# Two stage changes of a two-block network, worked in token halves

## The reference

```
# block 1
h = rms_norm(x) * gain * (1 + sc1) + sh1
y = hybrid_mixer(h)                       # gated convolution beside attention, then @ w_o
x = x + g1 * rms_norm(y, mix_post_g)      # stage change 1 begins with this line
h = rms_norm(x, ffn_pre_g) * (1 + sc2) + sh2
y = swiglu_ffn(h)                         # (silu(h @ wg) * (h @ wu)) @ w_ffn_out
x = x + g2 * rms_norm(y, ffn_post_g)      # stage change 2 begins with this line
# block 2
h = rms_norm(x, norm_g) * (1 + scale) + shift
y = mamba2_mixer(h)                       # h @ in_w, causal convolution, state space, @ out_w
...                                       # then an attention block and a last norm
```

## Time and profile before

| | |
|---|---|
| median of 3 runs | 1399.63 us (1399.52 to 1403.42) |
| the profiled execution | 1405.93 us, its span 1404.1 us |
| TensorE busy | 1342.2 us (96%) |
| VectorE / ScalarE / GpSimd busy | 823.6 (59%) / 588.5 (42%) / 407.2 (29%) |
| TensorE's granted clock over the run | 0.973 of full |
| DMA | 181 MB, mean 129 GB/s |

### The profile page before, as it was taken

The page is one execution under the profiler, slowest core; times in us unless marked ns, Lnnn a source line. Parts: engine busy times, 40 slices in busy tenths (PEclk is TensorE's granted clock), DMA queues, the critical chain, the costliest instruction groups (busy, mean ns, idle before and its releaser), DMA issues. The chain is left out here.

```text
span 1404.1 us, 19406 instructions
## 1 busy us (share of the span) xinstructions
PE 1342.2 (96%) x7840; PEld 1068.1 (76%) x7840; DVE 823.6 (59%) x966; ACT 588.5 (42%) x849; POOL 407.2 (29%) x191
## 2 busy tenths in 40 slices
PE   5999999889999999999999999999999999999996
PEld 3778867668888888887778886777786799777775
DVE  2789974476655654323766665777842842566644
ACT  4323646333222222112454347867732422455551
POOL 0000000039988888999100000000000050233310
PEclk9999999979999999999799999999999899999998
DMA  9434052215454445554132334333322342111121
GB/s 385 145 146 150 31 208 96 87 34 204 171 219 179 179 179 183 210 180 185 51 130 84 104 115 121 113 113 102 117 90 91 123 169 89 70 50 42 61 91 60
DMA packets 41350, 181.12 MB, mean 129 GB/s; under 512 B 3392, under 2 KB 20160, under 8 KB 21312
## 3 DMA queue, kind: packets, MB, share of 16 engines
q1 hardware_dynamic: 40128, 171.73, 33.9%
q10 hardware_dynamic: 1152, 8.39, 1.8%
HBM read 173.75 MB, written 6.36 MB: 128 GB/s over the span
## 5 line engine op out<-in xcount | busy, mean ns | idle before, releaser
L193 DVE TENSOR_TENSOR wlo<-raw,whi 128x2048 fp32r<-128x2048 f32 x95 | 257.1, 2707 | 172.0 <-ACT whi L189 169.4
L200 POOL TENSOR_TENSOR ada_raw<-ada_raw,cs 128x2048 f32<-128x2048 f32 x36 | 144.6, 4018 | 495.2 <-DVE h2lo L454 446.9
L271 PE MATMUL ps<-hhi,whi 128*128 128x512 f32 x640 | 252.0, 394 | 2.4 <-PEq L566 0.8
L271 PE MATMUL ps<-hhi,wlo 128*128 128x512 f32 x640 | 249.4, 390 | 0.0
L271 PE MATMUL ps<-hlo,whi 128*128 128x512 f32 x640 | 249.1, 389 | 0.0
L189 ACT ACTIVATE whi<-raw 128x2048 fp32r<-128x2048 f32 x95 | 181.6, 1911 | 141.7 <-PE ps L1315 91.3
L209 POOL TENSOR_TENSOR ada_raw<-ada_raw 128x1024 f32<-128x1024 f32 x72 | 166.0, 2305 | 5.6
L271 PEld LDWEIGHTS ps<-hhi,whi 128*128 128x128 f32 x640 | 120.2, 188 | 28.7 <-issue 2.4
L271 PEld LDWEIGHTS ps<-hhi,wlo 128*128 128x128 f32 x640 | 120.1, 188 | 25.6
L271 PEld LDWEIGHTS ps<-hlo,whi 128*128 128x128 f32 x640 | 120.3, 188 | 24.4
L2054 POOL TENSOR_TENSOR x<-x,rest 128x256 f32<-128x256 f32 (+3 forms) x32 | 49.1, 1533 | 153.2 <-DVE rest L2349 153.2
(11 more groups left out here) (374 smaller groups left out, 2760.6 us busy)
## 6 DMA issues: line engine op xcount, KB each, us to landing
raw<-panels SPq DMA_DIRECT2D x87, 1024.0 KB, 4.9
ada_raw<-ada SPq DMA_DIRECT2D x48, 1024.0 KB, 6.7
first<-ada SPq DMA_DIRECT2D x8, 1024.0 KB, 20.2
bc<-ac_rows SPq DMA_DIRECT2D x32, 256.0 KB, 3.7
raw<-panels ACTq DMA_DIRECT2D x8, 1024.0 KB, 5.0
x_kept<-x SPq DMA_DIRECT2D x2, 2048.0 KB, 9.5
x<-x_kept SPq DMA_DIRECT2D x2, 2048.0 KB, 8.3
x<-x_in SPq DMA_DIRECT2D x1, 2048.0 KB, 10.3
```

The costliest lines, as they stand in the source:

```text
L193: e.tensor_tensor(wlo[:, c % 2, :, :], raw[:, c % 2, :, :], whi[:, c % 2, :, :].bitcast(F32), ALU.subtract).then_inc(lo_split, 1)
L200: e.tensor_tensor(ada_raw[:, c % 2, :, :], ada_raw[:, c % 2, :, :], cs[:, which, :].unsqueeze(2).to_broadcast([P, KT, 256]), ALU.mult).the ...
L271: mm = e.matmul(ps[:, 2 * (qc % 2) + b, :], w[:, c % 2, 2 * k + b, :], src[part][:, k, :], **flags)
```

## The change

`post_norm` and `pre_norm` at the two stage changes are replaced by one function, `boundary`, that works over tokens 0 to 255 (a = 0) and then 256 to 511 (a = 1). Tiles 7 and 6 of the last panel stay whole; the other six are done for half 0 first and then for half 1, so 72 products of 256 columns stand for 36 of 512. Squares, sums, root, reciprocal and spread exist per half; four `keep` operations of 256 tokens are VectorE's, the six of half 1 ScalarE's. The scale and add steps handle two tiles of 256 tokens at once. The first **two** panels of the next stage are both in `boundary`: panel A half 0, panel B half 0 (with the second norm's sums and spread of half 1 between its products), panel A half 1, panel B half 1, 192 products of 256 columns. ScalarE rounds panel B in four parts between its `high` steps; VectorE's `split_lo` of panel B stands behind its `norm(0)`. The next blocks therefore begin with the third panel. The modulation columns are grouped 4, 4, 5 instead of 3, 3, 1, 1, 2, 3, the last five behind the last product.

```diff
+            def on_pe(pe, part, c, qc):
+                for j in range(2):
+                    part(TILES[j], slice(0, S)).then_inc(N["bank_done"], 1)
+                for j in range(2, KT):
+                    part(TILES[j], HALF[0]).then_inc(N["bank_done"], 1)
+                    for t in {4: (0, 1), 6: (2, 3, 4)}.get(j, ()):
+                        sums(pe, 0, t)
+                for j in range(2, KT):
+                    pe.wait_ge(*no("kept", j + 1))
+                    part(TILES[j], HALF[1]).then_inc(N["bank_done"] if j < KT - 1 else panels_used, 1)
+                    for t in {2: (5, 6, 7)}.get(j, ()):
+                        sums(pe, 0, t)
+                    for t in {3: (0, 1), 6: (2, 3, 4, 5)}.get(j, ()):
+                        sums(pe, 1, t)
+                    if j == 4:
+                        half_spread(pe, 0, 0, 7)
+                for t in (6, 7):
+                    sums(pe, 1, t)
+                columns(pe, 0)
+                half_spread(pe, 1, 1, 6)
+                for i in range(4):
+                    sums2(pe, 0, i)
+                columns(pe, 1)
+                half_spread(pe, 2, 0, 5)
+                pe.wait_ge(*no("x_new1", 2))
+                for a in range(2):
+                    for p in range(2):
...
+                            pe.wait_ge(lo_split, cp + 1)
...
+                            if (a, p) == (0, 1) and k == 3:
+                                for i in range(4):
+                                    sums2(pe, 1, i)
+                            if (a, p) == (0, 1) and k == 6:
+                                half_spread(pe, 3, 1, 7)
+                        if a == 1:
+                            mm.then_inc(panels_used, 1)
+                columns(pe, 2)
...
+                for k in range(KT):
+                    high(0, k)
+                    if k < 4:
+                        split_hi_part(act, last + 2, k)
+                for i in range(4):
+                    square2(1, i)
+                std(1, 7, 12)
+                for k in range(KT):
+                    high(1, k)
...
+                recip(1, 1)
+                dve.wait_ge(*no("spread", 2))
+                scale(1, 0, both(y, 0, 1))
+                recip(2, 0)
+                dve.wait_ge(*no("kept_b", 2))
+                scale(1, 1, both(y, 1, 1))
+                dve.wait_ge(*no("spread", 3))
+                dve.wait_ge(*no("x_new0", 2))
+                dve.wait_ge(*no("x_new1", 2))
+                norm(0)
                 split_lo(dve, last + 2, 0)
...
+                scale(1, 3, both(y, 3, 1))
+                add(1, 3, both(y, 3, 1))
+                recip(3, 1)
+                dve.wait_ge(*no("spread", 4))
...
+                norm(1)
...
                     def _(pe):
-                        pairs(pe, FT - 1, lambda i, r: (in_panel(pe, c0 + 1 + r, q0 + 1 + r, i, (hhi, hlo), False),
+                        pairs(pe, FT - 2, lambda i, r: (in_panel(pe, c0 + 2 + r, q0 + 2 + r, i, (hhi, hlo), False),
                                                         ada_columns(pe, a0 + r, i)))
+                        ada_columns(pe, a0, FT // 2 - 1)
...
-                        xbc_panel(0, 0)
                         xbc_panel(0, 1)
```

More of the change, by code:

```diff
@@ L371, in post_norm, with half_sums, sums @@
-            a0, a1, sums, parts = late or (0, 0, None, [0] * 6)
+            def half_sums(pe, a, bank, src, first, final):
+                for i in range(2):
+                    b = 2 * a + i
+                    mm = pe.matmul(ps[32 * b:32 * b + 32, bank, 0:P], ones[:, 0:32], src[:, i * P:(i + 1) * P], start=first,
+                                   stop=final, skip_group_check=True)
+                return mm
+            def sums(pe, a, j):
+                if j == 0:
+                    pe.wait_ge(*no("kept", a + 1))
+                pe.wait_ge(*no("sq_ready", j + 1 if j < 2 or a == 0 else j + 7))
+                half_sums(pe, a, 7 - a, sq[:, j % 3, HALF[a]], j == 0, j == KT - 1).then_inc(N[sums_of[a]], 1)
@@ L372, in post_norm @@
+            a0, a1, acc, parts = late or (0, 0, None, [0] * 3)
             assert sum(parts) == a1 - a0
@@ L415, in on_dve @@
+                for j in range(2):
+                    keep(j, slice(0, S))
+                split_lo(dve, last + 1, 0)
+                for j in range(2, KT):
+                    keep(j, HALF[0])
+                recip(0, 0)
                 dve.wait_ge(*no("kept", KT))
                 dve.wait_ge(*no("spread", 1))
-                for j, k in enumerate(ORDER):
-                    part = ps[:, SPARE[j], :] if j % 2 else y[:, k, :]
-                    dve.tensor_tensor(part, y[:, k, :], ps[:, ORDER[0], :], ALU.mult).then_inc(N["scaled"], 1)
-                    if j % 2:
-                        dve.wait_ge(*no("scaled", j + 1))
-                        dve.tensor_tensor(x[:, k, :], x[:, k, :], part, ALU.add).then_inc(N["x_new1"], 1)
@@ L1257, in _ @@
                             ada_reduce(pool, a, 0, sums(a))
[L1258 removed]
+                        step2["pool"](pool)
                     @block.scalar
```

266 lines of the change are left out of this document (179 added, 87 removed).

## The result

| | median | lowest to highest | profiled execution |
|---|---|---|---|
| before, 4 runs | 1399.58 us | 1398.45 to 1403.42 | 1405.93, span 1404.1 |
| after, 4 runs | 1436.36 us | 1435.42 to 1442.86 | 1436.47, span 1434.7 |

The ratio is 1.0268 [1.0232, 1.0304]: slower. The forecast was 1424.9 with a range of 1413 to 1434; the direction was right, and the range missed by 2.4 us. Between the two profiled executions the change costs 30.5 us, where 25.3 was forecast.

A forecast was written before the change was run, and what follows sets the result against it. TensorE sets the time nearly everywhere, its clock dipping at both stage changes. Stage change 1 (-1.1 panels, +10.7 idle, +2.4 clock = +12.0) and stage change 2 (+13.3) give +25.3 on 1399.6: 1424.9 us, range 1413 to 1434.

The forecast's parts named there:

- The restart: TensorE behind the new hole at each stage change: the clock falls and must rise again, +2.4 us, bounds 0 and 2.7.
- (1): Sign: first product of the next stage 5 to 8 us sooner after the last panel's start.
- (3): Sign: end of the second panel within 3 us of before, counted from the start of the last panel.
- (2): Sign: TensorE gaps behind panel B's `split_lo` and in panel A half 1, released by VectorE.
- (4): Sign: TensorE idle 10 to 11 us at the feed-forward block's start, 11 to 12 at the next, clock 0.5 after each.
- (5): Sign: the rest of the trace is merely shifted.
- Stage change 2 by the same steps: Panels end at 711.9, columns to 713.1, TensorE starts at 725.5 against 714.64: +10.9, clock +2.4, together +13.3 us.
- The step from the profile to the median: Before's profile is 6.3 us above its median, so +25.3 was added to 1399.6 instead, giving 1424.9 us.
- (a): Rival: no hold, ScalarE and VectorE run on once panel A is done; +6.6 to +11, 1406 to 1411 us; chance 4%.
- (b): Rival: faster or level, as the second panel's time was slack; 1396, with the clock up 1394 us; chance 3%.
- (c): Rival: hold, but TensorE well fed, panels end at 309.9; +7.2 per change, 1414 to 1415 us; chance 14%.
- (d): Rival: worse feeding, small operations and four roots dearer; +3 to +4.5 per change, 1431 to 1434 us; chance 12%.

The follow-up runs named there:

- before again: The kernel before, unchanged, profiled a second time; 1405.5 us.
- before, third and fourth profile, without the dip: The kernel before, unchanged, profiled twice more; the clock did not fall near 197 us; 1400.48 and 1400.24 us.
- after, second profile, without the dip: The kernel after, unchanged, profiled again; the clock did not fall near 197 us; 1433.46 us.
- border_moved: Kernel before, no halves, with only the second panel moved to the old block's end at both stage changes; 1430.23 us, ratio 1.0184.
- one_panel: Kernel after with panel B whole and back in the new block, the rest still in halves; 1416.38 us, ratio 1.0104.
- split_in_old_block: Kernel after with ScalarE's and VectorE's split of the third panel done in the old block; 1427.97 us.
- sums_ahead: Kernel after with the second sums of half 0 ahead of half 1's spread in TensorE's queue; 1437.22 us, ratio 1.0254.
- one_panel_sums_ahead: The queue edit of sums_ahead put on one_panel; 1411.29 us, ratio 1.0083.
- split_and_sums: The queue edit of sums_ahead put on split_in_old_block; 1428.51 us.
- one_panel_early_half: One-panel form, sums ahead, with the second half's norm brought under the first half's products; 1418.73 us, ratio 1.014.
- columns_late: Kernel after with the first two parts of the modulation columns moved behind the last product; one execution, 1439.2 us.
- after_hold_filled: Kernel after with 42 and 46 products of no use at the head of the two new blocks; 1430.55 us, ratio 1.0195.
- before_filled: Kernel before with 36 and 9 products of no use in TensorE's waits inside the two stage changes; 1397.74 us, ratio 0.997.
- experiment 10: The experiment that ran after_hold_filled, to see what the low clock costs; 1430.55 us.
- experiment 8: New profiles of unchanged kernels to test the clock's dip near 197 us: before 1400.48 and 1400.24 us, after 1433.46 us.

## Why the prediction was right or wrong

The stretches of the profiles not in the first table, in us, worked out from the four starts and the span:

| | start to keep 1 | keep 1 to silu | silu to keep 2 | keep 2 to memset | memset to end |
|---|---|---|---|---|---|
| before again | 261.5 | 44.4 | 352.8 | 44.2 | 700.8 |
| before, third and fourth profile, without the dip | 258.5, 258.1 | 44.7, 44.6 | 352.8, 352.8 | 43.1, 43.1 | 699.7, 700.0 |
| after, second profile, without the dip | 257.7 | 55.6 | 353.0 | 60.6 | 704.8 |
| border_moved | 261.2 | 55.3 | 353.8 | 54.7 | 704.6 |
| one_panel | 257.8 | 48.2 | 352.8 | 51.3 | 701.0 |
| split_in_old_block | 261.0 | 55.4 | 349.9 | 60.6 | 701.6 |
| sums_ahead | 261.1 | 54.4 | 353.8 | 61.9 | 702.7 |
| one_panel_sums_ahead | 257.2 | 44.8 | 352.8 | 49.1 | 701.1 |
| split_and_sums | 257.2 | 54.3 | 351.2 | 61.3 | 698.9 |
| one_panel_early_half | 261.0 | 48.3 | 354.2 | 49.5 | 701.7 |
| columns_late | 259.8 | 58.2 | 353.8 | 63.8 | 701.8 |
| after_hold_filled | 257.8 | 55.6 | 352.0 | 62.2 | 700.4 |
| before_filled | 259.1 | 41.1 | 352.8 | 42.4 | 699.8 |

*What held.* The reading that decides the sign: all engines are held at a block's end until TensorE is done, and the second panel was the cover for what follows. `border_moved` shows it with whole panels: 25.9 of the 30.5 us between profiles, its span 1429.6 against 1403.7 for the second profile of before. At stage change 1 the sums of the forecast came out. Brought to the same keep 1, the first product came at 285.3 (forecast 284.6), the end of the panels at 315.2 (314.7), the third panel's first matmul at 325.8 (325.4). All of it, up to keep 2, cost 11.2 + 0.4 = 11.6 us, with 12.0 forecast.

Part of that agreement is luck. The root behind the last sum, forecast at 276.1, starts at 277.9 on that scale (276.58, 16.4 us after keep 1), 1.8 late; the last product of the old stage ends at 275.8 and not at 273.9. Then 1.1 came back: the forecast has the sums and the spreads behind that root at the lower clock, and in this execution the clock stayed at the upper level until 283. Where it fell in time, in stage change 1 of `columns_late`, the first product is 3.3 us later than the steps say (26.45 for 23.15 after keep 1). The restart was too dear in the forecast as well: up to keep 2 only 1.6 us are left for it, where 2.4 was forecast, and filling the hole gave 1.0 to 1.2 back (experiment 10). And the rise at stage change 2 was misread: 0.67 in the microsecond from 694 puts it at 694.7, 6.0 and not 5.7 us after the first product, which changes the 2.4 by less than 0.1.

Of the signs named, (1), the first product 5 to 8 us sooner, holds at stage change 1 (5.6) and fails at stage change 2 (2.2). (3), the panels' end within 3 us of before, holds at both, 0.6 sooner and 2.2 later. (2) holds for panel B, which starts 0.1 us after its `split_lo` behind a gap of 1.3 us (1.2 at stage change 2) for which the profile names no releaser; in panel A half 1 the tiles come every 0.79 us, VectorE's pace, but the only gap that the profile names is of 0.2 us and put down to ScalarE's `hhi`. (4) holds for the first idle time, 10.5 us; the second, 12.6 us, is longer than the 11 to 12 named. (5), the rest merely shifted, does not hold: the short dip at 972 us (experiment 10) is new.

*The step that failed: "Stage change 2 by the same steps".* It was forecast at 13.3 us. In the first two profiles it is 16.1 up to the memset and 4.1 behind it, 20.2, so 6.9 more.

- The first product came 4.6 us later than the steps say (23.15 after the keep forecast, 27.8 measured), the panels' end 4.3. Three terms were too small. The root behind the last sum starts 16.6 us after keep 2 (685.56) where 14.65 was forecast, 1.9 late; that error stage change 1 has too. The columns I let go on in the hole as before, at no cost. There they lay in a hole with room; in the halved chain they stand in TensorE's queue ahead of both spreads, and these start 1.3 and 0.5 us after their reciprocal was done, where it is 0.1 at stage change 1: 1.7 us. And four sums at the lower clock, taken at 2.2 to 2.5 us, are 3.63, 1.3 more. The second spread, at the upper clock again, gave 0.3 back.
- The columns behind the last product take 2.3 us (726.63 to 728.9), 1.1 more than forecast. The five entries are two matmuls each, and the trace has two instructions of 0.12 for each of these: 20, as the 4 and 16 in the rows show. The hole itself, 12.0 from the memset to the matmul for 11.6, and 0.2 less for the change of blocks, add 0.2.
- Behind the hole 3.7 instead of 2.4. The restart of this execution is 2.9 (experiment 10), and 1.6 is the short dip at 972 us, which both profiles of the kernel after and those of `border_moved` and `split_in_old_block` have, and those of before, `sums_ahead`, `columns_late` and `after_hold_filled` have not. The remaining -0.8 is in the main a norm near 1088 us, which costs 0.9 more in the first profile of before than in its third.

*The step from the profile to the median.* I took the 25.3 from a profile 6.3 us above the median and added them to the median. That assumes that the 6.3 belong to every execution of either kernel alike. They are made of places where one execution has the clock down and the next has not (experiment 8), and the kernel after has its own: its 1433.46 without the dip at 197 lies 2.9 below its median of 1436.36. Against the executions without the dip the change costs 33.1, so the forecast of its cost is 7.8 short: 5.6 from the first two points (4.3, 1.1 and 0.2), 1.3 from the third, 1.2 because stage change 2 of before itself takes 43.1 there and not 44.3, and -0.3 in sum of smaller differences of both signs. The median of the kernel after then lies higher still by what its executions have of such dips. That last part, 2.9 us, is read from four times and one profile and is not settled. A range to 1434 had room for the sum's bounds but none for this.

*The rivals.* (a) is excluded by `border_moved`, and (b) with it. By the Trainium skill, "Trainium Architecture — The Big Picture", section "What this means for kernel authors", only a semaphore makes one engine wait for another. That alone does not foretell the hold: the kernel writes no such wait at a block's end, and the profile still names TensorE's queue as what released ScalarE there (PEq L749 in `border_moved`). The isolated gap between matmuls that the Trainium skill gives in "TensorE: Matmul & The Clock Gate", section "Back-to-back issue gap", would have made the forecast smaller by 3.7 us. The trace does not bear it out: the matmuls of 256 columns of the kernel after start 0.12 us apart too. (c), a well-fed pair of panels, would have shown the panels' end at 309.9; it was 315.2 on the same scale. (d), small operations dearer than interpolated, gives a time near the right one, 1431 to 1434, for a reason that the trace does not show: VectorE's and ScalarE's operations at 256 columns came within 0.1 us of the estimates, 0.79 us a tile for the 0.8 I took.

*What halving is worth by itself.* With the border in its old place, one panel in halves is 3.8 and 6.9 us slower than the first profile of before (48.2 and 51.3 against 44.4 each), 3.5 and 8.2 slower than the profiles without the dip. Half 1 needs its own sums, root, reciprocal and spread, 6.6 us without a product, and stage change 2 adds the columns. That the second panel covers the second half's chain is the one gain of taking it along, and it costs the cover behind the border: 10.5 and 12.6 us of standing still.

Why the clock fell before the sums at stage change 2 and after them at stage change 1 of the same execution stays open. TensorE was busy for 2.44 of 4 us from 276, where the clock stayed up, and for 2.94 of 4 us from 684, where it fell, so it is not simply the idler place that falls first.

## What to carry to other kernels

Before work is moved across the end of a block, look for what the moved piece covers on the other side: if all engines start together when the slowest is done, the first wait of the new block is paid in full unless its own engine brings work along. When a chain is halved, list every instruction that stands in the queue between its links, for work that lay in a roomy hole becomes part of the chain. Where TensorE must stand still in a chain of sums and spreads, products of no use in its waits can pay (0.3% here, with not one needed instruction changed), and a profile that lies above the median should be taken again until it is known in which stretch.

## What the runs showed of the hardware

- In places where TensorE works with gaps the granted clock differs from one execution to the next. The same instructions near 197 us ran with 0.63 or 1.00 in a window of 5 us, and the end of that stage came 3.0 to 3.4 us later or earlier; the second sums of stage change 1 took 2.05 or 3.63 us.
- Matmuls of one column with a weight load each cost as much as those of 256 columns: 16 took 1.93 us with the clock up (0.12 each) and 3.58 with it down (0.22 each); those of 256 columns start 0.12 and 0.21 apart.
- Filling TensorE's waits pays twice: the second spread of the chain takes 1.16 us for 2.08, and the first product behind a filled hole 0.49 for 0.79.
